# Two-block model on one core: rope angles moved from GpSimd to VectorE, and the border between the gates' run and the output projection rearranged

## What is computed

```python
for i in range(DEPTH):                       # 2 layers
    u = rms_norm(h, norm_g[i])
    z = u @ w_in[i]                          # queries, keys, values, gates g_a, g_b, g_c
    o_a = mla_mixer(...)                     # 6 heads
    o_b = dsa_mixer(...)                     # 5 heads over the top 64 keys of an index score
    o_c = diff_mixer(...)                    # 5 heads, then rms_norm with subln_g
    mixed = concat([o_a * silu(g_a), o_b * silu(g_b), o_c * silu(g_c)])
    h = h + mixed @ w_o[i]
    h = h + (p[i] @ w_ple[i]) * sigmoid(h @ w_pg[i])
```

## Time and profile before

| | |
|---|---|
| median of 3 runs | 3248.19 us (3245.33 to 3252.24) |
| profiled execution | 3248.7 us; span 3247.0 us from first to last instruction |
| mean granted TensorE clock | 0.98 |
| TensorE, VectorE, ScalarE, GpSimd busy | 95%, 74%, 42%, 10% |
| HBM | 216 GB/s over the span |

### The profile page before, as it was taken

One profiled execution on the slowest core, in us unless ns is written; L12 is line 12 of the kernel. 1 busy time (PEld: TensorE's weight loads), 2 busy tenths in 40 slices (PEclk: granted clock), 3 DMA queues, 4 the chain that ended last, 5 costly groups with the idle time before them and its releaser, 6 DMA issues.

```text
span 3247.0 us, 58745 instructions
## 1 busy us (share of the span) xinstructions
PE 3080.3 (95%) x24402; PEld 2947.3 (91%) x24402; DVE 2399.3 (74%) x3298; ACT 1369.0 (42%) x1470; POOL 333.5 (10%) x556
## 2 busy tenths in 40 slices
PE   5999999999999989999999999999999999899998
PEld 5997889989978889999999999998689999799998
DVE  5887888888877878875766676677877986567464
ACT  3334453443344544443443334434744333434342
POOL 7110000001000000000001010100000322010000
PEclk9999999999999999999999999999999999899999
DMA  4875446767754477575767674776166765386563
GB/s 185 279 283 180 169 158 246 260 213 281 280 187 163 159 270 256 202 254 195 274 207 279 237 276 167 274 266 229 58 216 225 227 207 188 122 289 235 206 221 130
DMA packets 130953, 710.48 MB, mean 219 GB/s; under 512 B 16393, under 2 KB 16545, under 8 KB 71585
## 3 DMA queue, kind: packets, MB, share of 16 engines
q1 hardware_dynamic: 67392, 484.47, 42.6%
q0 software_dynamic: 61264, 214.93, 18.8%
q10 hardware_dynamic: 2064, 7.70, 0.6%
HBM read 700.26 MB, written 2.10 MB: 216 GB/s over the span
## 4 chain that ended last, share of the span: by engine, by line
PE 79%; DVE 11%; ACT 4%; issue 3%; DMA 2%; POOL 2%; ACTq 0%; DVEq 0%; POOLq 0%
PE bank L553 24%; PE bank L549 21%; PE bank L550 21%; DVE wlo L1640 3%; ACT whi L1089 2%; PE bank L654 2%; DVE aslab L1665 2%; DMA aslab<-w_ada_dram 2%; DVE sc L1759 1%; PE bank L883 1%; PE bank L602 1%; PE bank L664 1%; PE bank L997 1%; PE bank L904 1%; DVE yc L2301 1%
## 5 line engine op out<-in xcount | busy, mean ns | idle before, releaser
L549 PE MATMUL bank<-uhi,whi 128*128 128x256 f32 x6720 | 1664.4, 287 | 68.0 <-ACT whi L1089 18.0
L550 PE MATMUL bank<-ulo,whi 128*128 128x256 f32 x6720 | 1647.9, 285 | 0.0
L1089 ACT CAST whi<-raw 128x2048 fp32r<-128x2048 f32 (+1 forms) x464 | 875.7, 1890 | 1544.7 <-PE bank L553 1488.1
L1640 DVE TENSOR_TENSOR wlo<-raw,whi 128x2048 fp32r<-128x2048 f32 (+1 forms) x464 | 1056.8, 2279 | 575.7 <-ACT whi L1089 575.1
L549 PEld LDWEIGHTS bank<-uhi,whi 128*128 128x128 f32 x6720 | 1303.0, 194 | 80.7 <-issue 51.5
L550 PEld LDWEIGHTS bank<-ulo,whi 128*128 128x128 f32 x6720 | 1303.2, 194 | 2.9 <-issue 2.4
L553 PE MATMUL bank<-uhi,wlo 128*128 128x256 f32 x6720 | 885.9, 284 | 13.2 <-DVE wlo L1640 13.2
L553 PEld LDWEIGHTS bank<-uhi,wlo 128*128 128x128 f32 x6720 | 841.1, 192 | 18.0 <-DVE wlo L1640 15.3
L462 POOL DMA_DIRECT2D aslab<-w_ada_dram x384 | 203.1, 529 | 2652.3 <-DVE mod L1665 1437.1
L1665 DVE CUSTOM_DVE_ANT_0 aslab<-aslab,sil,part 128x1024 f32<-128x1024 f32 x192 | 245.4, 1281 | 42.6 <-DMA aslab<-w_ada_dram 42.5
L1665 DVE CUSTOM_DVE_ANT_0 aslab<-aslab,sil,cols 128x1024 f32<-128x1024 f32 x192 | 245.3, 1280 | 42.7 <-DMA aslab<-w_ada_dram 42.7
(11 more groups left out here) (270 smaller groups left out, 2417.5 us busy)
## 6 DMA issues: line engine op xcount, KB each, us to landing
aslab<-w_ada_dram POOLq DMA_DIRECT2D x384, 512.0 KB, 5.1
raw<-w_win_dram SPq DMA_DIRECT2D x96, 1024.0 KB, 4.9
raw<-w_wfi_dram SPq DMA_DIRECT2D x96, 1024.0 KB, 5.0
raw<-w_wfo_dram SPq DMA_DIRECT2D x48, 1024.0 KB, 4.9
raw<-w_wci_dram SPq DMA_DIRECT2D x48, 1024.0 KB, 5.2
raw<-w_wo_dram SPq DMA_DIRECT2D x32, 1024.0 KB, 5.4
raw<-w_wpg_dram SPq DMA_DIRECT2D x32, 1024.0 KB, 5.1
raw<-w_wqz_dram SPq DMA_DIRECT2D x32, 1024.0 KB, 4.9
```

The source lines that it names most:

```text
L549: nc.tensor.matmul(o, w_, xhi_, start=start, stop=False, skip_group_check=True)
L550: nc.tensor.matmul(o, w_, xlo_, start=False, stop=False, skip_group_check=True)
L1089: nc.scalar.copy(whi[:, s % 2, 0:n], raw[:, s, 0:n]).then_inc(s_hi, 1)
L1640: v.tensor_tensor(wlo[:, s, 0:n], raw[:, s, 0:n], whi[:, s % 2, 0:n].bitcast(F32), ALU.subtract).then_inc(s_lo, 1)
```

## The change

1. The angles are computed on VectorE, as its first instructions after the inputs have landed: a cast, three multiplies, and for cosine and sine 8 instructions of 768 columns each (multiply and add are one instruction). POOL's 26 instructions go, and its loads follow one another.
2. `ada_due`: `ga` has its 16 pieces in its first 13 slabs (two each at slabs 4, 8 and 12, none at 13 to 15); `qz` has 36, 20 over its first 16 slabs and then one a slab; `attn2` has 16, one every second unit.
3. The half slabs of `ple` lie in four places, two to each place of `whi` (`half_slot`). All four are split by ScalarE and VectorE before `ple` begins.
4. ScalarE fills quarter 0 of `mixed` at its step 13 and quarter 1 at step 15, and takes the square roots in the unit steps 22 and 23. VectorE makes quarter 0 at its step 14 and p at step 15, before the first reciprocal; quarter 1 and half slabs 2 and 3 follow it, then the second reciprocal.
5. Slab 0 of w_o is split by ScalarE after the third drain of `ple`, slab 1 after the fourth; VectorE splits slab 0 before the last gates and slab 1 after.

```diff
@@ stream_plan, ada_due
-            run("qz", "T", "wqz", 0, 8, ada=40)
-            run("attn2", "A", None, 0, 0, ada=12)
+            run("qz", "T", "wqz", 0, 8, ada=36)
+            run("attn2", "A", None, 0, 0, ada=16)
-        if r["name"] in ("pg1", "fco", "fxo"):
+        if r["name"] in ("ga0", "ga1", "pg1", "fco", "fxo"):
             return r["ada"] * min(p, 13) // 13
+        if r["name"] == "qz":
+            return 20 * min(p, 16) // 16 + max(0, p - 16)
@@ the places of the half slabs
+        def half_slot(s):
+            return whi[:, s % 2, 1024 * (s // 2):1024 * (s // 2) + 1024]
@@ TensorE, ple
-                            last = mm3(o, whi[:, s % 2, wc], wlo[:, s, wc], uhi[:, 8 + k, :], ulo[:, 8 + k, :],
+                            last = mm3(o, half_slot(s)[:, wc], wlo[:, s, wc], uhi[:, 8 + k, :], ulo[:, 8 + k, :],
@@ ScalarE
                     unit_step(t)
+                    if t == N1 + 1:
+                        subln_root(0, bank[5])
+                    if t == N1 + 2:
+                        subln_root(1, bank[6])
+                        subln_root(2, bank[7])
...
+                def split_half(s):
+                    act.wait_ge(s_raw[s], 16 * (r["m0"] + 1))
+                    act.wait_ge(s_slab, SLABS * r["m0"] - 1 + s % 2)
+                    nc.scalar.copy(half_slot(s), raw[:, s, 0:1024]).then_inc(s_hi, 1)
...
-                        split(r, 0, q - 14)
+                        split_half(q - 14)
+                    if q == 13:
+                        act.wait_ge(s_aw, 2 * l + 2)
+                        act.wait_ge(s_slab, SLABS * ga["m0"] + 13)
+                        fill_quarter(f"m{l}", zz_t, 0)
...
+                    if q == 15:
+                        act.wait_ge(s_of, NT1 * l + 13)
+                        fill_quarter(f"m{l}", zz_t, 1)
...
-                act.wait_ge(s_aw, 2 * l + 2)
-                act.wait_ge(s_of, NT1 * (l + 1))
-                fill_quarter(f"m{l}", zz_t, 0)
-                for c in range(3):
-                    subln_root(c, bank[5 + c])
-                fill_quarter(f"m{l}", zz_t, 1)
+                split_half(2)
+                split_half(3)
...
                 for s in range(SLABS):
-                    if s + 2 < SLABS:
-                        split(r, 0, s + 2)
-                    elif s == 2:
-                        presplit(f"o{l}")
                     drain_e(s)
+                    if s >= 2:
+                        split(RUN[f"o{l}"], 0, s - 2)
@@ VectorE, at its start (the same lines go from GpSimd, with two instructions for each scalar_tensor_tensor)
             dve.wait_ge(s_in, 16 * INPUT_DMAS)
+            link(v.tensor_copy(ang[:, 0:T], posi[:, :]))
+            for k in (2, 1, 0):
+                last = v.tensor_scalar(ang[:, T * k:T * (k + 1)], ang[:, 0:T],
+                                       kk[:, K_INVF + k:K_INVF + k + 1], None, ALU.mult)
+            link(last)
...
+            for i, (turn, back) in enumerate(((0.25, math.pi / 2), (0.0, 0.0))):
+                x = red[i][:, :]
+                link(v.tensor_scalar(trn[:, :], ang[:, :], 1 / TWO_PI, turn, ALU.mult, ALU.add))
+                link(v.tensor_scalar(trn[:, :], trn[:, :], ROUND, None, ALU.add))
+                link(v.tensor_scalar(trn[:, :], trn[:, :], -ROUND, None, ALU.add))
+                for c, y in ((C1, ang[:, :]), (C2, x), (C3, x)):
+                    link(v.scalar_tensor_tensor(out=x, in0=trn[:, :], scalar=-c, in1=y,
+                                                op0=ALU.mult, op1=ALU.add))
+                link(v.tensor_scalar(x, x, back, PI32, ALU.add, ALU.min))
+                v.tensor_scalar(x, x, -PI32, None, ALU.max).then_inc(s_sin, 1)
@@ VectorE, the border
-                        split(r, 0, q - 14)
+                        split_half(q - 14)
+                    if q == 14:
+                        fill_quarter(f"m{l}", zz_t, 0)
+                    if q == 15:
+                        fill_u(f"p{l}", praw[:, :, :].rearrange("p k n -> p (k n)"), 1, 512, 4, 2048)
                     point(2 * q + 2)
                     ada(ga, q)
-                fill_u(f"p{l}", praw[:, :, :].rearrange("p k n -> p (k n)"), 1, 512, 4, 2048)
-                fill_quarter(f"m{l}", zz_t, 0)
-                dve.wait_ge(s_ort, 3 * l + 1)
-                link(v.reciprocal(ort[:, 0:512], ort[:, 0:512]))
-                split(r, 0, 2)
+                    if q == 15:
+                        dve.wait_ge(s_ort, 3 * l + 1)
+                        link(v.reciprocal(ort[:, 0:512], ort[:, 0:512]))
                 fill_quarter(f"m{l}", zz_t, 1)
+                split_half(2)
+                split_half(3)
                 dve.wait_ge(s_ort, 3 * l + 3)
                 link(v.reciprocal(ort[:, 512:1280], ort[:, 512:1280]))
-                split(r, 0, 3)
+                split(RUN[f"o{l}"], 0, 0)
...
-                presplit(f"o{l}")
+                split(RUN[f"o{l}"], 0, 1)
```

More of the change, by code:

```diff
@@ L258, in build @@
         red = [sb(f"red{i}", 3 * T, at=place["trn"] + 3 * T * 4 * (i + 1)) for i in range(2)]
-        turns = sb("turns", 3 * T, at=place["trn"] + 3 * T * 4 * 3)
         cc_t = sb("cc", KT * T, at=arena)
@@ L356, in build @@
         s_sin = sem("table_angle_ready")
-        s_ang = sem("table_steps")
         s_tab = sem("tables_ready")
@@ L475, in _ @@
             cond(0)
-            done = [0]
-            def follow(ins):
-                done[0] += 1
-                ins.then_inc(s_ang, 1)
-                pool.wait_ge(s_ang, done[0])
-            pool.wait_ge(s_in, 16 * INPUT_DMAS)
-            follow(nc.gpsimd.tensor_copy(ang[:, 0:T], posi[:, :]))
-            for k in (2, 1, 0):
-                last = nc.gpsimd.tensor_scalar(ang[:, T * k:T * (k + 1)], ang[:, 0:T],
-                                               kk[:, K_INVF + k:K_INVF + k + 1], None, ALU.mult)
-            follow(last)
-            TWO_PI = 2 * math.pi
-            C1 = 6.28125
-            C2 = float(np.float32(np.round((TWO_PI - C1) * 2 ** 20) / 2 ** 20))
-            C3 = TWO_PI - C1 - C2
-            ROUND = 12582912.0
-            PI32 = 3.1415925
-            for i, (turn, back) in enumerate(((0.25, math.pi / 2), (0.0, 0.0))):
-                x = red[i][:, :]
-                follow(nc.gpsimd.tensor_scalar(trn[:, :], ang[:, :], 1 / TWO_PI, turn, ALU.mult, ALU.add))
-                follow(nc.gpsimd.tensor_scalar(trn[:, :], trn[:, :], ROUND, None, ALU.add))
-                follow(nc.gpsimd.tensor_scalar(trn[:, :], trn[:, :], -ROUND, None, ALU.add))
-                for c, y in ((C1, ang[:, :]), (C2, x), (C3, x)):
-                    follow(nc.gpsimd.tensor_scalar(turns[:, :], trn[:, :], -c, None, ALU.mult))
-                    follow(nc.gpsimd.tensor_tensor(x, turns[:, :], y, ALU.add))
-                follow(nc.gpsimd.tensor_scalar(x, x, back, PI32, ALU.add, ALU.min))
-                nc.gpsimd.tensor_scalar(x, x, -PI32, None, ALU.max).then_inc(s_sin, 1)
             at = 2
@@ L1862, in _ @@
             dve.wait_ge(s_in, 16 * INPUT_DMAS)
+            link(v.tensor_copy(ang[:, 0:T], posi[:, :]))
[3 more added lines that the diff above has]
+            link(last)
+            TWO_PI = 2 * math.pi
+            C1 = 6.28125
+            C2 = float(np.float32(np.round((TWO_PI - C1) * 2 ** 20) / 2 ** 20))
+            C3 = TWO_PI - C1 - C2
+            ROUND = 12582912.0
+            PI32 = 3.1415925
+            for i, (turn, back) in enumerate(((0.25, math.pi / 2), (0.0, 0.0))):
[8 more added lines that the diff above has]
+                v.tensor_scalar(x, x, -PI32, None, ALU.max).then_inc(s_sin, 1)
             def lambda_products():
@@ L2084, in first_block, with split_half @@
                 ga, r = RUN[f"ga{l}"], RUN[f"ple{l}"]
+                ort = zz_t[:, T * Z_ORT:T * (Z_ORT + 5)]
+                def split_half(s):
+                    dve.wait_ge(s_hi, SLABS * r["m0"] + s + 1)
+                    v.tensor_tensor(wlo[:, s, 0:1024], raw[:, s, 0:1024], half_slot(s).bitcast(F32),
+                                    ALU.subtract).then_inc(s_lo, 1)
                 for q in range(16):
```

1 line of the change is left out of this document (removed).

## The result

The changed kernel takes **3214.25 us** (median of 4 executions, 3211.14 to 3215.11) for 3247.16 beside it (3245.33 to 3252.24): a ratio of 0.9894, 95% interval 0.9878 to 0.9909, so 1.06% faster. The forecast was 3210, range 3198 to 3224. The profiled execution took 3213.67 us around a span of 3212.0; of before, 3248.7 around 3247.0. So 35.0 us went, where I had summed 38.3.

A forecast was written before the change was run, and what follows sets the result against it. TensorE was busy 95% of the span, so only its idle time and lower-clock matmuls could shrink. Terms -15.7 + 9.0 - 28.0 - 3.6 = -38.3 took 3248.7 to 3210.4 us, 3210 by the median; range 3198 to 3224.

The forecast's parts named there:

- Head: Layer 0's first run without POOL's angles becomes layer 1's, 14.1 us less, and the gap before it 1.6 less: -15.7 us.
- The chain's size: Angles on VectorE at the start: about 15.6 us, ending near 25.8, before the norm's reciprocal at 32.13; cost 0.
- Layer 1 as a model for layer 0: First run: same work in both layers, 200.5 us in layer 0 and 186.4 in layer 1; layer 0 should match.
- The rival that gave the head only 5.6: Head's first slabs wait for weights or SP, not only POOL: 5.6 us in place of 15.7, total 3220; chance 0.12.
- The three pieces: Three pieces a layer moved forward within `ga`: cost +4.5 us a layer, +9.0 in all; bounds 0 and +15.
- slab 12 is free and slabs 4 and 8 aren't: Extra pieces in `ga`: the first two cost 2.0 and 2.5 us, the third falls where VectorE waits for TensorE.
- The rival "hidden": The pieces moved forward in `ga` cost nothing, since VectorE is idle 18 us there: total 3201; chance 0.18.
- The border: From `ga`'s last slab to the end of w_o's slab 0: 22.1 us for 35.6 and 36.6, together -28.0.
- the first wait: Before `ple`, after `ga`'s last slab: TensorE waits 3.1 us for half slab 1 and p, not 5.5.
- late transfer of w_o: SP's second w_o load could be late at some 360 GB/s: bounds 0 and +3 us a layer.
- the 1.5 us for the lower clock: Within the border's 22.1 us: 1.5 us for the first matmuls running at the lower clock.
- Attention: `qz` and `attn2`: attention starts 1.2 us earlier, the even schedule saves 2.4; together -3.6, bounds -5 and +5.

The follow-up runs named there:

- e4: Changed kernel with the angles of rope back on POOL, as before the change, all else as changed: 3229.66 us.
- e3: Changed kernel with VectorE making the low part of p before the low half of weight slab 1 at slab 15: 3210.51 us.
- e1: Changed kernel with the pieces of the gates' two runs even again, one per slab: 3212.25 us.
- e7: Changed kernel with the gates' pieces still further forward, 16 in the first ten slabs and none after: 3227.88 us.
- e9: Changed kernel with gates' second pieces at slabs 0 and 3, none at 8 and 15; p's low part first; last gates drain before quarter 1; layer 1's silu late: 3194.67 us.
- e12: e9 unchanged, measured again as the pair of a run with attention's pieces as before: 3203.08 us.
- e2: Changed kernel with the gates' pieces even, but that of slab 15 put to slab 0: 3203.65 us.
- e10: e1 with layer 1's silu of the condition moved behind the low rank step's drains: 3202.76 us.

## Why the prediction was right, and where it was off

**Head: right.** The forecast was -15.7; the traces show -15.45 up to `v` and -15.6 up to the gates, and undoing the part costs 15.4, with the reserve told under e4. The chain's size was off to the safe side: 12.9 us for my 15.6, because 768 columns take 0.56 and 0.96 us for my 0.72 and 1.0. Layer 1 as a model for layer 0 held to 0.1 us. The rival that gave the head only 5.6 falls. Its bound was too low because it counted the wait of 4.0 behind the late piece and not the one of 4.98 ahead of it; the stretched instructions by themselves come nearer to 8.7 than to the lower end at which I had put them.

**The three pieces: right cause, size too small.** +4.5 a layer was forecast and 5.7 measured. The step that failed counted TensorE's waits alone. Its idle time in the gates' window grew from 2.1 us (140.50 - 138.41) to 6.0 (146.20 - 140.22), 3.9 for my 4.5; what I left out are 1.8 us more busy time, matmuls at the lower clock behind those waits. Two windows of the changed kernel show the clock below 1.00 there (length, PE busy, clock, DMA, GB/s):

```profile
424.80:427.80 3.00, 2.88 (x13) 0.69 0.47 142
427.80:437.40 9.60, 7.90 (x58) 0.92 0.51 177
```

I had priced the lower clock in the border and forgotten it here. How much it takes varies: layer 0 of e3, with the same pieces and 6.1 us idle, has 0.7 us more busy time than before, not 1.8. That slab 12 is free and slabs 4 and 8 aren't was right: the new waits for VectorE stand at 400, 410 and 425, ahead of slab 12's pieces; the one behind them, 1.74, was 1.48 before. The rival "hidden" falls by e1, where the even schedule takes the gates back to 140.4, and by e7, where the same work still earlier costs 7 us more.

**The border: right.** -28.0 was forecast, -28.6 measured: 22.4 and 21.2 us for my 22.1; the first wait 3.05 for 3.1; `o` 0.18 behind the low rank step for 0.2; no late transfer of w_o. Of the 1.5 us for the lower clock some 1.2 came in layer 0 (0.90 up to w_o) and none in layer 1 (1.00). What I did not see is why layer 1 needs the pieces early: the load of the conditions behind the last piece (e1). I gave the early pieces a cost in the gates and no such benefit; the sum was right since I took the change whole.

**Attention: too large.** -3.6 was forecast: 1.2 of an earlier start and 2.4 by the schedule. The schedule gave 1.9 between units 2 and 31. The rest did not come. From attention's first matmul to unit 2 it is 9.8 us (2211.20 to 2220.99) for 10.0 (2246.04 to 2256.03), though TensorE's first wait in it fell from 3.78 to 2.64; and the stretch from the norm ahead of the query run to attention took 242.9 us for 239.2, in waits for low parts behind late pieces.

**Not in the sum:** -2.7 in the output projections, -1.1 in layer 1, +3.6 in later stages, of which 2.1 is one wait for a load. They cancel to -0.2, and that is luck: the 3.2 us between -38.3 and -35.1 are then in the main the pieces (2.4) and attention (1.5), less 0.6 of the border. Ten of the eleven traces with the new attention schedule have such a wait there and one of the three with the old; the same kernel had none as e9 and one as e12. I can't tie it to the change.

## What to carry to other kernels

Filler work has its price by place, not by amount: at slab 0 a second piece cost nothing, at slabs 4 and 8 two of them cost 3.9 us of waits for their 5.0 and, in most runs, the clock behind these, and its best place is found by looking where the filled engine already waits for the one that bounds. Before moving it, ask which loads and which other engine's steps are queued behind its last instruction; in layer 1 that was worth 6.5 us of border and no view of TensorE's waits of before showed it. And where an identical stage ran twice, the quicker one was here the better estimate of what the slower can become (186.4 us for 186.4), and a sum of the waits that were named gave 5.6 of 15.5 us.

## What the runs showed that I had not expected

The same wait of 3.05 us before the low rank step was followed by the lower clock in layer 0 and by none in layer 1: from the gates' end to w_o the granted clock is 0.90 and 1.00, with 13.3 and 12.0 us of busy time for the same matmuls:

```profile
465.90:482.39 16.49, 13.26 (x98) 13.09 (x97) 13.49 (x8) 11.41 (x15) 0.00 (x0) 0.90 0.56 196
1114.20:1129.55 15.35, 12.02 (x97) 11.64 (x97) 13.50 (x8) 13.07 (x16) 0.00 (x0) 1.00 0.81 314
```

In layer 0 the matmuls after the wait start 0.12 us apart for 1.4 us, then 0.21 apart, then 0.12 again: full and half speed, 2.4 and 1.2 GHz, in the middle of unbroken work. e2 has 0.90 in both layers with the same wait, e4 in the other layer. A wait of this length thus comes with 0 or some 1.2 us more busy time behind it, and no run shows what decides it; that is as much as several of the terms argued over here. And the DMA engines moved 350 to 369 GB/s over 16 to 18 us in layer 1 of e10 and e9, where before it was 274 in the same stretch (1134.52 to 1163.89); ScalarE's waits for w_o stayed under 2 us, 1.6 at most.
